# Strassen's block product for half of an output projection, with VectorE making the remainders of its weights

## The chip, the cores and the metric

The kernel runs on one core of a Trainium2 chip. The metric is the device time of one execution in microseconds (us), the median of several executions. All tensors are float32. "TensorE" does the matmuls (PE in the profile), "VectorE" is DVE, "ScalarE" is ACT, "GpSimd" is POOL, "SyncE" (SP) issues the loads and stores of this kernel.

## The reference

One layer of a hybrid mixer over 512 tokens of width 2048: a norm, one input projection of 2048 by 7168, two groups of heads (a gated recurrence and a convolution, each giving 1024 channels), one output projection of 2048 by 2048, a norm of its result and the residual. The change touches the last two lines only.

```python
h = rmsnorm(x, pre_norm_g[l])
proj = jnp.einsum('btd,dn->btn', h, w_in[l])
q, fz, iv, gate_a, u, ug, gate_b = jnp.split(proj, split_pts, axis=-1)
o_a = hgrn2_mixer(q, fz, iv, lower_bounds[l], hg_norm_g[l]) * jax.nn.silu(gate_a)
o_b = conformer_conv(u, ug, dw_kernel[l], dw_bias[l], conv_ln_g[l], conv_ln_b[l]) * jax.nn.silu(gate_b)
mixed = jnp.concatenate([o_a, o_b], axis=-1)          # (1, 512, 2048)
y = jnp.einsum('btm,md->btd', mixed, w_out[l])        # w_out: (2048, 2048)
x = x + rmsnorm(y, post_norm_g[l])
```

## The kernel before

Every engine has a program of its own, written out in order; the engines wait for each other on semaphores (`wait_ge(sem, n)`), and nothing is reordered.

**Products in three parts.** To keep float32 accuracy each operand of a projection is split in a rounded part (`hi`, type fp32r) and the remainder (`lo = value - hi`), and each product is made of three matmuls: hi by hi, hi by lo, lo by hi.

**Units of weights.** The weights of both projections come in units of 128 partitions by 1024 elements (512 KB). A unit n goes through a ring of four slots in three tensors: SyncE loads `w_raw`, ScalarE copies it into `w_hi` (`hi_unit`, L386, which waits for the load and for the unit n - 4 to be used up, `unit_done`), GpSimd makes `w_lo = w_raw - w_hi` (`lo_unit`, L333, `lo_done`), and TensorE uses both. SyncE's load of unit n waits for `lo_done` of unit n - 4.

**The output projection** goes over four chunks c of 512 columns of `w_out`, and in each over eight units s (`OUT_U`), each with 256 of the 2048 mixed channels (in the order of `PAIRS`, the channels that are ready first coming first). A unit is 24 matmuls of 128 rows, 128 channels and 512 columns (`out_products`): four tiles tt of 128 tokens, two channel blocks, three matmuls. Chunk c is summed in PSUM banks 4 * (c % 2) + tt. The last four units of the last chunk are gone through tile by tile, so that tile 0 is whole first.

**The left operand** is made during chunk 0: the mixed channels lie in `mix`, transposed (channels on the partitions, 512 tokens along), ScalarE rounds them block by block into `h_hi` (`mix_hi`, L625) and VectorE makes `h_lo` (`mix_lo`, L1022, `mlo_done`). Unit s of chunk 0 waits for `mlo_done` of 2s + 2 blocks. Between them VectorE still works on the last head and the last convolution tile: `late(H - 1, ...)` and `ln_tile`; the last block of `mix`, which is head 7, comes out of `late` at s == 7 (L990, L993), so the chain L990, L993, `mix_hi(15)`, `mix_lo(15)` ends just ahead of unit 7 of chunk 0.

**After a chunk** ScalarE squares and sums each bank (`take_sq`, L636, `y_sq`) and VectorE writes the bank times the norm's gain into `mix` (`take_y`, L1032). After the last chunk, for each tile in turn: ScalarE squares; VectorE adds the four sums (L1053) and does `take_y`; ScalarE makes the root (L672, L674); VectorE writes y * root + x over the tile (L1059, one instruction of 2048 columns, in the last tile four of 512); SyncE stores it (1 MB, the last tile in four parts).

Of the kernel before, what the change touches and what calls it, by code (L numbers as in the profile page):

```python
# [27 lines left out]
def build_layer(nc, x, pre_norm_g, post_norm_g, w_in, lb_logits, hg_norm_g, dw_kernel, dw_bias,  # L28
# [3 lines left out]
    ds = bass.ds  # L32
# [59 lines left out]
    with ctx:  # L92
# [16 lines left out]
        def part(n, k=1):  # L109
            return work[:, n * T:(n + k) * T]  # L110
# [49 lines left out]
        def h_pair(h, th, k):  # L160
# [74 lines left out]
        def _(sp):  # L235
            def load_unit(n, slot, src, width):
                sp.dma_start(w_raw[:, slot * UW:(slot + 1) * UW].rearrange("p (k c) -> p k c", c=width),
                             src.rearrange("(k p) c -> p k c", p=P)).then_inc(raw_in[slot], 16)
# [49 lines left out]
            with sp.Fori(0, H) as h:  # L288
                for u in range(HEAD_U):
# [4 lines left out]
                    in_unit(n, u % RING, u % 2, HEAD_COLS[u // 2] + h * P)  # L294
            with sp.Fori(0, CHUNKS) as c:
                for s in range(OUT_U):
                    n = N_OUT + OUT_U * c + s
                    cut_before = held(sp, n - RING + 1)
                    sp.wait_ge(raw_in[s % RING], 16)
                    sp.wait_ge(lo_done, cut_before)  # L300
                    load_unit(n, s % RING, w_out[0, 2 * P * PAIRS[s]:2 * P * (PAIRS[s] + 1), ds(c * 512, 512)], 512)
            parts = 0
# [9 lines left out]
        def _(pool):  # L312
# [55 lines left out]
            g.memset(probs, 0.0).then_inc(masks_ready, 1)  # L368
            with pool.Fori(PEEL, N_END // RING) as i:
                for s in range(RING):  # L370
                    lo_unit(RING * i + s, s)


        @block.scalar
        def _(act):
# [250 lines left out]

            def take_sq(c, tt):


                if c < CHUNKS - 1:  # L630
                    act.wait_ge(y_taken, TT * c + tt + 1)
                else:
                    act.wait_ge(y_mm, (TT - 1) * c + tt + 1)
                if c:
                    act.wait_ge(y_sq, TT * (c - 1) + tt + 1)
                A(part(tt), bank(4 * (c % 2) + tt), ACT.Square, accum_out=ssq[:, tt * CHUNKS + c:tt * CHUNKS + c + 1]).then_inc(y_sq, 1)  # L636

            def out_hi(c, s):
                n = N_OUT + OUT_U * c + s + AHEAD
                if n < N_END:  # L640
                    hi_unit(n, n % RING, n // RING)
# [16 lines left out]
            for c in range(1, CHUNKS):  # L658
                for s in range(OUT_U):
                    out_hi(c, s)  # L660
                    if c == 1 and s == 0:

                        act.wait_ge(mlo_done, KT)
                        for tt in range(TT):
                            act.dma_start(work[:, 4 * T + tt * D:4 * T + (tt + 1) * D], x[0, tt * P:(tt + 1) * P, :]).then_inc(res_in, 16)
                    if s in (1, 2):
                        take_sq(c - 1, 2 * s - 2)
                        take_sq(c - 1, 2 * s - 1)
# [9 lines left out]
        def _(dve):  # L678
# [344 lines left out]

            def take_y(c, tt):

                if c == CHUNKS - 1:
                    dve.wait_ge(y_sq, TT * c + tt + 1)
                elif tt < TT - 1:
                    dve.wait_ge(y_mm, (TT - 1) * c + tt + 1)
                else:  # L1030
                    dve.wait_ge(unit_done, N_OUT + OUT_U * (c + 1))
                V.tensor_tensor(mix[:, tt * D + c * 512:tt * D + (c + 1) * 512], bank(4 * (c % 2) + tt),  # L1032
                                gates[:, c * 512:(c + 1) * 512], ALU.mult).then_inc(y_taken, 1)

            for at in range(4):
                mix_lo(at)
            for s in range(OUT_U):
# [6 lines left out]
                for at in {2: (6, 7), 3: (8, 9), 4: (10, 11), 5: (12, 13), 6: (14,), 7: (15,)}.get(s, ()):  # L1044
                    mix_lo(at)
            dve.wait_ge(gain_in, 32)
            for c in range(CHUNKS - 1):
                for tt in range(TT):
                    take_y(c, tt)
            dve.wait_ge(res_in, 16 * TT)  # L1050
            for tt in range(TT):
                dve.wait_ge(y_sq, TT * (CHUNKS - 1) + tt + 1)
                V.tensor_reduce(rst[:, TT + tt:TT + tt + 1], ssq[:, tt * CHUNKS:(tt + 1) * CHUNKS], AX.X, ALU.add).then_inc(y_ssum, 1)  # L1053
                take_y(CHUNKS - 1, tt)
                dve.wait_ge(y_rs, 2 * (tt + 1))
                dve.wait_ge(y_taken, TT * (CHUNKS - 1) + tt + 1)
                for a, b in out_parts(tt):
                    y = mix[:, tt * D + a:tt * D + b]
                    V.scalar_tensor_tensor(y, y, rst[:, tt:tt + 1], work[:, 4 * T + tt * D + a:4 * T + tt * D + b],  # L1059
                                           ALU.mult, ALU.add).then_inc(y_out, 1)  # L1060


        @block.tensor
        def _(pe):
# [221 lines left out]

            def out_products(c, s, tt):
                for k in range(2):
                    a = slice((2 * s + k) * T + tt * P, (2 * s + k) * T + (tt + 1) * P)
                    w = slice((s % RING) * UW + k * 512, (s % RING) * UW + (k + 1) * 512)  # L1290
                    o = bank(4 * (c % 2) + tt)
                    mm(o, h_hi[:, a], w_hi[:, w], start=s == 0 and k == 0, stop=False)  # L1292
                    mm(o, h_hi[:, a], w_lo[:, w], start=False, stop=False)  # L1293
                    ins = mm(o, h_lo[:, a], w_hi[:, w], start=False, stop=s == OUT_U - 1 and k == 1)  # L1294
                return ins

            for c in range(CHUNKS):
                for s in range(OUT_U):
                    n = N_OUT + OUT_U * c + s
                    if N_END - n <= RING:  # L1300
                        break
                    if c == 0:
                        slot(H - 1, s, False, last=True)
                    if c == 0 and s == 0:
                        pe.wait_ge(gb_taken, H)
                    if s == 0 and c >= 2:
                        pe.wait_ge(y_sq, TT * (c - 1))
                    pe.wait_ge(lo_done, n + 1)
                    if c == 0:
                        pe.wait_ge(mlo_done, 2 * s + 2)  # L1310
                    for tt in range(TT):
                        if (c, s, tt) == (0, 0, 1):
                            pe.wait_ge(gate_taken, H)
                        ins = out_products(c, s, tt)
                        if s == OUT_U - 1 and tt < TT - 1:
                            ins.then_inc(y_mm, 1)
                    ins.then_inc(unit_done, 1)

            for tt in range(TT):
                for s in range(OUT_U - RING, OUT_U):  # L1320
                    pe.wait_ge(lo_done, N_END - OUT_U + s + 1)
                    ins = out_products(CHUNKS - 1, s, tt)
                ins.then_inc(y_mm, 1)
# [22 lines left out]
```

## Time and profile before

| | |
|---|---|
| three timed executions | 880.49, 880.89, 882.67 us; median 880.89 us |
| the profiled execution | 880.39 us, of which its span on the core is 878.4 us |
| TensorE busy | 867.4 us, 99% of the span |
| VectorE, ScalarE, GpSimd busy | 558.2 us, 389.5 us, 364.2 us |
| chain that ended last | TensorE 99% |

The span is the time between the first and the last recorded instruction or transfer; 2 us of the device's time lie outside it. A busy share is an average over stages: in the output projection VectorE is nearly unused between the chunks.

### The profile page before, as it was taken

The numbers are of one execution on the slowest core, as the hardware profiler recorded it, in microseconds if no ns is written. First come the engines' busy times: TensorE is split into PE (matmuls) and PEld (weight loads), VectorE is DVE, ScalarE is ACT, GpSimd is POOL, SyncE is SP. The second block draws the span as 40 slices with busy tenths as digits, with TensorE's granted clock in tenths as the row PEclk, the third lists the DMA queues.
The fourth block names the chain that finished last, engine by engine and source line by source line (L and its number), as shares of the span: only waits on it lengthen the run. The fifth ranks groups of instructions, "written<-read, shape, count | busy, mean of one in ns | idle before, by whom it ended". The sixth has DMA issues, their size and how long they took to land.

```text
span 878.4 us, 12378 instructions
## 1 busy us (share of the span) xinstructions
PE 867.4 (99%) x4258; PEld 727.5 (83%) x4258; DVE 558.2 (64%) x929; ACT 389.5 (44%) x617; POOL 364.2 (41%) x165
## 2 busy tenths in 40 slices
PE   8999999999999999999999999999999999999996
PEld 7988888888888888888888888888888888888885
DVE  4697788788678993957758395775939882010105
ACT  7522213323323466646646564664656653222221
POOL 4284444444444444342524434253443443444440
PEclk9999999999999999999999999999999999999998
DMA  9253333333333323141331324133131336433304
GB/s 311 80 145 98 97 99 101 97 101 100 97 98 98 95 64 97 58 121 49 96 96 51 105 59 119 48 96 96 48 105 62 110 131 234 143 99 99 96 1 191
DMA packets 115899, 89.76 MB, mean 102 GB/s; under 512 B 2672, under 2 KB 101273, under 8 KB 114585
## 3 DMA queue, kind: packets, MB, share of 16 engines
q1 hardware_dynamic: 115113, 84.04, 31.5%
q10 hardware_dynamic: 752, 5.25, 1.6%
q8 instruction: 23, 0.38, 0.2%
q14 instruction: 11, 0.09, 0.0%
HBM read 85.09 MB, written 4.19 MB: 102 GB/s over the span
## 4 chain that ended last, share of the span: by engine, by line
PE 99%; DVE 0%; ACT 0%; POOL 0%; issue 0%; DVEq 0%; ACTq 0%; POOLq 0%
PE banks L1155 19%; PE banks L1157 19%; PE banks L1156 19%; PE banks L1292 7%; PE banks L1293 7%; PE banks L1294 7%; PE banks L1170 3%; PE banks L1171 3%; PE banks L1172 3%; PE banks L1101 3%; PE banks L1213 1%; PE banks L1203 1%; PE banks L1219 1%; PE banks L1072 1%; PE banks L1247 1%; PE banks L1222 1%
## 5 line engine op out<-in xcount | busy, mean ns | idle before, releaser
L333 POOL TENSOR_TENSOR w_lo<-w_raw,w_hi 128x1024 fp32r<-128x1024 f32 x144 | 358.1, 2490 | 487.3 <-ACT w_hi L386 486.9
L1155 PE MATMUL banks<-h_hi,w_hi 128*128 128x512 f32 x736 | 291.1, 396 | 0.0
L1157 PE MATMUL banks<-h_hi,w_lo 128*128 128x512 f32 x736 | 286.7, 390 | 0.0
L1156 PE MATMUL banks<-h_lo,w_hi 128*128 128x512 f32 x736 | 286.5, 389 | 0.0
L386 ACT ACTIVATE w_hi<-w_raw 128x1024 fp32r<-128x1024 f32 x144 | 151.9, 1055 | 263.5 <-PE banks L1294 100.1
L745 DVE SCALAR_TENSOR_TENSOR banks<-work,tap,banks 128x512 f32<-128x512 f32 x232 | 175.3, 756 | 8.0
L1157 PEld LDWEIGHTS banks<-h_hi,w_lo 128*128 128x128 f32 x736 | 138.1, 188 | 29.3
L1156 PEld LDWEIGHTS banks<-h_lo,w_hi 128*128 128x128 f32 x736 | 138.3, 188 | 28.1 <-issue 0.5
L1155 PEld LDWEIGHTS banks<-h_hi,w_hi 128*128 128x128 f32 x736 | 138.2, 188 | 28.0 <-issue 0.5
L1292 PE MATMUL banks<-w_hi,h_hi 128*128 128x512 f32 x256 | 100.6, 393 | 0.0
L1294 PE MATMUL banks<-w_hi,h_lo 128*128 128x512 f32 x256 | 99.7, 389 | 0.0
L1293 PE MATMUL banks<-w_lo,h_hi 128*128 128x512 f32 x256 | 99.6, 389 | 0.0
L1032 DVE TENSOR_TENSOR mix<-banks,gates 128x512 f32<-128x512 f32 x16 | 11.0, 689 | 85.6 <-PE banks L1294 85.6
L1294 PEld LDWEIGHTS banks<-w_hi,h_lo 128*128 128x128 f32 x256 | 48.0, 188 | 10.1
L1292 PEld LDWEIGHTS banks<-w_hi,h_hi 128*128 128x128 f32 x256 | 48.1, 188 | 10.1 <-issue 0.2
L1293 PEld LDWEIGHTS banks<-w_lo,h_hi 128*128 128x128 f32 x256 | 48.1, 188 | 10.0 <-issue 0.2
L1170 PE MATMUL banks<-w_hi,h_hi 128*128 128x512 f32 x128 | 49.8, 389 | 0.0
L1171 PE MATMUL banks<-w_lo,h_hi 128*128 128x512 f32 x128 | 49.8, 389 | 0.0
L1172 PE MATMUL banks<-w_hi,h_lo 128*128 128x512 f32 x128 | 49.8, 389 | 0.0
L946 DVE COPY_PREDICATED work<-mask,banks 128x192 f32<-128x192 int8 (+2 forms) x48 | 14.6, 303 | 27.5 <-PE banks L1213 20.2
L1172 PEld LDWEIGHTS banks<-w_hi,h_lo 128*128 128x128 f32 x128 | 24.0, 188 | 5.0
L1170 PEld LDWEIGHTS banks<-w_hi,h_hi 128*128 128x128 f32 x128 | 24.0, 188 | 5.0
(180 smaller groups left out, 906.2 us busy)
## 6 DMA issues: line engine op xcount, KB each, us to landing
w_raw<-in_w_in SPq DMA_DIRECT2D x112, 512.0 KB, 3.7
w_raw<-in_w_out SPq DMA_DIRECT2D x32, 512.0 KB, 3.7
work<-in_x ACTq DMA_DIRECT2D x4, 1024.0 KB, 10.0
out_y<-mix SPq DMA_DIRECT2D x3, 1024.0 KB, 3.9
mix<-in_x SPq DMA_DIRECT2D x4, 512.0 KB, 5.3
mix<-in_x SPq DMA_DIRECT2D x2, 1024.0 KB, 9.7
gates<-in_post_norm_g ACTq DMA_DIRECT2D x1, 1024.0 KB, 5.7
out_y<-mix SPq DMA_DIRECT2D x4, 256.0 KB, 2.7
```

Of the source, the lines that this page charges most:

```text
L333: g.tensor_tensor(w_lo[:, a], w_raw[:, a], w_hi[:, a].bitcast(fp32), ALU.subtract).then_inc(lo_done, 1)
L386: A(w_hi[:, a], w_raw[:, a], ACT.Copy).then_inc(hi_done, 1)
L745: V.scalar_tensor_tensor(dst, src, tp[:, w:w + 1], acc, ALU.mult, ALU.add).then_inc(tap_done, 1)
L1155: mm(bank(b), wh, hh, start=kt == 0, stop=False)
L1156: mm(bank(b), wh, hl, start=False, stop=False)
L1157: ins = mm(bank(b), wl, hh, start=False, stop=kt == KT - 1)
L1170: mm(o, h_hi[:, a], w_hi[:, w], start=vu == 0 and k == 0, stop=False)
L1171: mm(o, h_hi[:, a], w_lo[:, w], start=False, stop=False)
L1172: ins = mm(o, h_lo[:, a], w_hi[:, w], start=False, stop=vu == 2 * VH - 1 and k == VK - 1)
L1292: mm(o, h_hi[:, a], w_hi[:, w], start=s == 0 and k == 0, stop=False)
L1293: mm(o, h_hi[:, a], w_lo[:, w], start=False, stop=False)
L1294: ins = mm(o, h_lo[:, a], w_hi[:, w], start=False, stop=s == OUT_U - 1 and k == 1)
```

## The change

Columns 0 to 511 (chunk 0) are done as before, with GpSimd's remainders. Columns 512 to 1023 are ordinary too (units `C0` to `C7`). For columns 1024 to 2047 the product of `mixed` (512 tokens by 2048 channels) and `w_out` (2048 by 1024) is cut in two by two blocks and done with seven block products instead of eight (`P1` to `P7`, in Winograd's form with sums that are reused): each has 256 tokens, 1024 channels and 512 columns, and four steps u of 12 matmuls. `STEPS` sets the order: P1 (4 steps), C0, P2 (4), P5 (4), then for P6, P7, P3, P4 in turn two steps, one C, two steps, and last C5, C6, C7, again tile by tile. P products are summed in banks 4 and 5 or 6 and 7, C in banks 0 to 3.

New work around it: `sum_sides` (VectorE, in place on `mix`, 12 instructions, 9 of them inside chunk 0) makes the sums of the left operand; `side_rounded` (ScalarE) and `side_rest` (VectorE) split them; `sum_weights` (VectorE, 16) makes the sums of weights in four buffers `bsum` or in `w_raw`; `fast_rest` (VectorE) makes `w_lo` for all steps but the first two, in GpSimd's place; `keep` (ScalarE) and `join`, L1308 (VectorE) add up the block products; `gain` multiplies. Four more loads of 512 KB bring the first weights for `bsum` during chunk 0. The residual x is loaded later, at P4, over `mix`. The final write of a tile is four instructions of 512 columns for all tiles.

The core of the diff:

```diff
+    STEPS = [("P1", u) for u in range(HU)] + [("C", 0)] + [("P2", u) for u in range(HU)] + [("P5", u) for u in range(HU)]
+    for at, kind in enumerate(("P6", "P7", "P3", "P4")):
+        STEPS += [(kind, 0), (kind, 1), ("C", at + 1), (kind, 2), (kind, 3)]
+    LAST_C = [("C", s) for s in range(5, OUT_U)]
+    STEPS += LAST_C
+    SUM_PARTS = ((0, 4), (4, 2), (6, 2))
...
+            act.wait_ge(joined, JOINED["c21"])
+            for tt in (0, 1):
+                square(2, 2 + tt, pair_c21[:, tt * 512:(tt + 1) * 512])
             for tt in range(TT):
-                take_sq(CHUNKS - 1, tt)
+                act.wait_ge(y_mm, TT - 1 + tt + 1)
+                square(1, tt, bank(tt))
+            for tt in range(TT):
                 act.wait_ge(y_ssum, tt + 1)
                 A(rst[:, tt:tt + 1], rst[:, TT + tt:TT + tt + 1], ACT.Ln, scale=1.0 / D, bias=EPSB).then_inc(y_rs, 1)
...
+            def sum_sides(n, at):
+                i, k = SUM_PARTS[at]
+                if n == 0:
+                    out, a, b, op = low(i, k, EARLY), low(i, k, EARLY), low(i, k, LATE), ALU.subtract
...
+                dve.wait_ge(mlo_done, i + k + (KT // 2 if n else 0))
+                if n:
+                    dve.wait_ge(m_summed, M_SUM[n - 1, at])
+                V.tensor_tensor(out, a, b, op).then_inc(m_summed, 1)
...
+            def fast_rest(m):
+                kind, u = STEPS[m]
+                src = bsum[u] if kind in ("P5", "P6", "P4") else raw_of((kind, u))
+                a = slice(m % RING * UW, (m % RING + 1) * UW)
+                dve.wait_ge(hi_done, N_FAST + m + 1)
+                V.tensor_tensor(w_lo[:, a], src, w_hi[:, a].bitcast(fp32), ALU.subtract).then_inc(fast_lo, 1)
...
                 for at in {2: (6, 7), 3: (8, 9), 4: (10, 11), 5: (12, 13), 6: (14,), 7: (15,)}.get(s, ()):
                     mix_lo(at)
+                if s == 4:
+                    for at in range(3):
+                        sum_sides(0, at)
+                    for n in (1, 2, 3):
+                        sum_sides(n, 0)
+                if s == 6:
+                    for n in (1, 2, 3):
+                        sum_sides(n, 1)
+            for m, (kind, u) in enumerate(STEPS):
+                if m + 1 < len(STEPS) and STEPS[m + 1][0] in AHEAD_SUM:
+                    sum_weights(*STEPS[m + 1])
+                if (kind, u) in SIDE:
+                    side_rest(kind, u)
+                if m >= 2:
+                    fast_rest(m)
...
             for tt in range(TT):
                 dve.wait_ge(y_sq, TT * (CHUNKS - 1) + tt + 1)
                 V.tensor_reduce(rst[:, TT + tt:TT + tt + 1], ssq[:, tt * CHUNKS:(tt + 1) * CHUNKS], AX.X, ALU.add).then_inc(y_ssum, 1)
-                take_y(CHUNKS - 1, tt)
+                take_y(1, tt, y1[:, tt * 512:(tt + 1) * 512], bank(tt))
                 dve.wait_ge(y_rs, 2 * (tt + 1))
...
-                for a, b in out_parts(tt):
+                for c, y in enumerate(y_parts(tt)):
+                    out_c = mix[:, tt * D + c * 512:tt * D + (c + 1) * 512]
+                    ins = V.scalar_tensor_tensor(out_c, y, rst[:, tt:tt + 1], out_c, ALU.mult, ALU.add)
...
+            for m, (kind, u) in enumerate(STEPS[:-len(LAST_C)]):
+                pe.wait_ge(lo_done, N_FAST + m + 1) if m < 2 else pe.wait_ge(fast_lo, m - 1)
```

VectorE's program in chunk 0, before. The first row is the end of the last convolution tile; L1022 are `mix_lo` of blocks 10 to 14 and, in the row behind L993, 15; L990 and L993 end head 7; L1032 takes chunk 0 out of PSUM.

```order
L825 TENSOR_TENSOR mix<-work 128x512 [waits ln_v,ln_sig]
L1022 TENSOR_TENSOR h_lo<-mix,h_hi 128x512 [waits mhi_done] x5
L990 TENSOR_TENSOR work<-banks,work 128x512 [waits rs_s]
L993 SCALAR_TENSOR_TENSOR mix<-work,par 128x512 [waits gate_ready,on_done]
L1022 TENSOR_TENSOR h_lo<-mix,h_hi 128x512 [waits mhi_done]
L1032 TENSOR_TENSOR mix<-banks,gates 128x512 [waits y_mm,gain_in]
L1032 TENSOR_TENSOR mix<-banks,gates 128x512 [waits y_mm] x2
L1032 TENSOR_TENSOR mix<-banks,gates 128x512 [waits unit_done]
```

The same place now. L980 is the old L825, L1177 the old L1022, L1145 and L1148 the old L990 and L993; L1200 is `sum_sides`, L1215 `sum_weights` for P1, L1241 `fast_rest`.

```order
L980 TENSOR_TENSOR mix<-work 128x512 [waits ln_v,ln_sig]
L1177 TENSOR_TENSOR h_lo<-mix,h_hi 128x512 [waits mhi_done] x2
L1200 TENSOR_TENSOR mix<-mix 128x4x256 [waits mlo_done]
L1200 TENSOR_TENSOR mix<-mix 128x2x256 [waits mlo_done] x2
L1200 TENSOR_TENSOR mix<-mix 128x4x256 [waits m_summed,mlo_done] x3
L1177 TENSOR_TENSOR h_lo<-mix,h_hi 128x512 [waits mhi_done] x3
L1200 TENSOR_TENSOR mix<-mix 128x2x256 [waits m_summed,mlo_done] x3
L1145 TENSOR_TENSOR work<-banks,work 128x512 [waits rs_s]
L1148 SCALAR_TENSOR_TENSOR mix<-work,par 128x512 [waits gate_ready,on_done]
L1177 TENSOR_TENSOR h_lo<-mix,h_hi 128x512 [waits mhi_done]
L1215 TENSOR_TENSOR work<-work,w_raw 128x1024 [waits raw_in0,first_in0,lo_done]
```

Six sums now stand ahead of `mix_lo` of blocks 12 to 14, and three more ahead of the end of head 7.

ScalarE's program at its end, before (two of the four tiles; L636 squares, L672 and L674 make the root):

```order
L636 ACTIVATE work,ssq<-banks 128x512 [waits y_sq,y_mm]
L672 ACTIVATE rst<-rst,epsb 128x1 [waits y_ssum]
L674 ACTIVATE rst<-rst 128x1 [waits y_rs]
L636 ACTIVATE work,ssq<-banks 128x512 [waits y_sq,y_mm]
L672 ACTIVATE rst<-rst,epsb 128x1 [waits y_ssum]
```

The same place now (L733 squares, L827 and L829 make the root):

```order
L733 ACTIVATE near,ssq<-work 128x512 [waits y_sq,joined]
L733 ACTIVATE near,ssq<-work 128x512 [waits y_sq]
L733 ACTIVATE near,ssq<-banks 128x512 [waits y_sq,y_mm] x4
L827 ACTIVATE rst<-rst,epsb 128x1 [waits y_ssum]
L829 ACTIVATE rst<-rst 128x1 [waits y_rs]
L827 ACTIVATE rst<-rst,epsb 128x1 [waits y_ssum]
```

The squares of all four tiles now stand ahead of the first tile's root.

## Rows read from the trace of the kernel before

**Rows 1.** The page: the chain that ended last, by engine.

```profile
PE 99%; DVE 0%; ACT 0%; POOL 0%; issue 0%; DVEq 0%; ACTq 0%; POOLq 0%
```

**Rows 2.** Timeline of ScalarE: start us, us, instruction [idle before <-releaser].

```profile
728.56 1.06 ACT L386 ACTIVATE w_hi<-w_raw 128x1024 fp32r<-128x1024 f32 x1 [4.95 <-PE banks L1294]
...
732.76 0.63 ACT L625 ACTIVATE h_hi<-mix 128x512 fp32r<-128x512 f32 x1 [1.90 <-DVE mix L993]
...
762.11 1.06 ACT L386 ACTIVATE w_hi<-w_raw 128x1024 fp32r<-128x1024 f32 x1 [4.38 <-PE banks L1294]
767.55 1.06 ACT L386 ACTIVATE w_hi<-w_raw 128x1024 fp32r<-128x1024 f32 x1 [4.38 <-PE banks L1294]
```

**Rows 3.** Timeline of TensorE: units 6 and 7 of chunk 0, and the end.

```profile
729.40 0.40 PE L1293 MATMUL banks<-w_lo,h_hi 128*128 128x512 f32 x1
...
734.65 0.39 PE L1292 MATMUL banks<-w_hi,h_hi 128*128 128x512 f32 x1
...
740.09 0.39 PE L1292 MATMUL banks<-w_hi,h_hi 128*128 128x512 f32 x1
...
870.42 0.39 PE L1294 MATMUL banks<-w_hi,h_lo 128*128 128x512 f32 x1
```

**Rows 4.** Timeline of VectorE in chunk 0.

```profile
697.82 2.88 DVE L962 TENSOR_TENSOR work<-work 128x512 f32<-128x512 f32 x1
...
716.75 5.30 DVE L1022 TENSOR_TENSOR h_lo<-mix,h_hi 128x512 fp32r<-128x512 f32 x5
730.89 0.69 DVE L990 TENSOR_TENSOR work<-banks,work 128x512 f32<-128x512 f32 x1 [8.84 <-ACT work L587]
731.62 1.04 DVE L993 SCALAR_TENSOR_TENSOR mix<-work,par 128x512 f32<-128x512 f32 x1
733.42 0.69 DVE L1022 TENSOR_TENSOR h_lo<-mix,h_hi 128x512 fp32r<-128x512 f32 x1 [0.76 <-ACT h_hi L625]
```

**Rows 5.** Timeline of GpSimd in chunk 0.

```profile
697.30 2.84 POOL L333 TENSOR_TENSOR w_lo<-w_raw,w_hi 128x1024 fp32r<-128x1024 f32 x1
...
717.21 2.49 POOL L333 TENSOR_TENSOR w_lo<-w_raw,w_hi 128x1024 fp32r<-128x1024 f32 x1 [2.90 <-ACT w_hi L386]
722.64 2.40 POOL L333 TENSOR_TENSOR w_lo<-w_raw,w_hi 128x1024 fp32r<-128x1024 f32 x1 [2.94 <-ACT w_hi L386]
729.70 2.42 POOL L333 TENSOR_TENSOR w_lo<-w_raw,w_hi 128x1024 fp32r<-128x1024 f32 x1 [4.65 <-ACT w_hi L386]
```

**Rows 6.** Groups by line and shape from 700 us on: busy us, mean ns.

```profile
L1059 DVE SCALAR_TENSOR_TENSOR mix<-mix,rst,work 128x2048 f32<-128x2048 f32 x3 | 7.1, 2351 | 0.3
...
L1059 DVE SCALAR_TENSOR_TENSOR mix<-mix,rst,work 128x512 f32<-128x512 f32 x4 | 2.7, 747 | 0.1
```

**Rows 7.** Timeline of ScalarE at the end, last tile.

```profile
870.85 0.60 ACT L636 ACTIVATE work<-banks 128x512 f32<-128x512 f32 x1 [4.00 <-PE banks L1294]
...
871.76 0.29 ACT L672 ACTIVATE rst<-rst,epsb 128x1 f32<-128x1 f32 x1 [0.23 <-DVE rst L1053]
```

**Rows 8.** Timeline of VectorE at the end, last two tiles.

```profile
866.98 2.35 DVE L1059 SCALAR_TENSOR_TENSOR mix<-mix,rst,work 128x2048 f32<-128x2048 f32 x1
871.57 0.16 DVE L1053 TENSOR_REDUCE rst<-ssq 128x1 f32<-128x4 f32 x1 [2.23 <-ACT work L636]
...
872.43 2.74 DVE L1059 SCALAR_TENSOR_TENSOR mix<-mix,rst,work 128x512 f32<-128x512 f32 x4
```

**Rows 9.** Landings of the residual's four loads (L665), then of weights (L237), 720 to 760 us.

```profile
DMA to landing us min/median/max: 5.0/10.0/14.0
...
DMA to landing us min/median/max: 3.6/3.8/10.5
```

**Rows 10.** Stretches: length, busy us of PE (matmuls), PEld, DVE, ACT, POOL, granted clock, DMA.

```profile
2.00:4.00 2.00, 2.00 (x11) 2.00 (x10) 0.14 (x1) 0.10 (x1) 0.06 (x1) 1.00 0.84 242
...
6.00:7.00 1.00, 1.00 (x12) 1.00 (x11) 0.00 (x0) 0.90 (x2) 0.00 (x0) 1.00 0.94 344
...
872.50:873.00 0.50, 0.00 (x0) 0.00 (x0) 0.50 (x1) 0.00 (x0) 0.00 (x0) 0.81 0.14 49
```

More of the change, by code:

```diff
@@ L125, in build_layer @@
         glu = kdec
+        pair_c11, pair_c22 = part(0, 2), part(2, 2)
+        bsum = [part(4 + 2 * u, 2) for u in range(HU)]
+        pair_c21 = part(16, 2)
+        sides = sb("sides", [P, 2 * SIDES * T], fp32r)
+        side_hi = [sides[:, 2 * r * T:(2 * r + 1) * T] for r in range(SIDES)]
+        side_lo = [sides[:, (2 * r + 1) * T:(2 * r + 2) * T] for r in range(SIDES)]
+        y1 = part(12, TT)
+        pair_c12 = part(18, 2)
+        y0 = gates[:, D:2 * D]
         grow = work[0:KT, 0:P]
@@ L638, in out_hi, with square @@
[L638 to L641, printed above, removed]
+            squares = [0]
+            def square(c, tt, y):
+                if squares[0]:
+                    act.wait_ge(y_sq, squares[0])
+                squares[0] += 1
+                A(near[:, 0:512], y, ACT.Square, accum_out=ssq[:, tt * CHUNKS + c:tt * CHUNKS + c + 1]).then_inc(y_sq, 1)
+            def out_hi(s):
+                n = N_OUT + s + AHEAD
+                if n < N_FAST:
+                    hi_unit(n, n % RING, n // RING)
+                else:
+                    fast_hi(n - N_FAST)
@@ new lines, in side_rounded, with keep @@
+            def side_rounded(kind, u):
+                i = SIDE[kind, u]
+                act.wait_ge(m_summed, M_SUM[SUM_OF[kind], max(0, u - 1)])
+                if i >= SIDES:
+                    prev = [step for step in SIDE if SIDE[step] == i - SIDES][0]
+                    act.wait_ge(unit_done, N_FAST + AT[prev] + 1)
+                A(side_hi[i % SIDES].rearrange("p (k t) -> p k t", k=2), side(kind, u), ACT.Copy).then_inc(side_his, 1)
+            def keep(step, pair, b):
+                act.wait_ge(unit_done, N_FAST + AT[step] + 1)
+                A(pair, bank(b, 2), ACT.Copy).then_inc(kept, 1)
@@ new lines, in join, with gain @@
+            def join(step, out, b, pair, joins=0):
+                dve.wait_ge(unit_done, N_FAST + AT[step] + 1)
+                if joins:
+                    dve.wait_ge(joined, joins)
+                for n in range(2):
+                    a = slice(n * 512, (n + 1) * 512)
+                    V.tensor_tensor(out[:, a], bank(b + n), pair[:, a], ALU.add).then_inc(joined, 1)
+            def gain(c, pair, sq):
+                dve.wait_ge(y_sq, sq)
+                dve.wait_ge(gain_in, 32)
+                for n in range(2):
+                    a = slice(n * 512, (n + 1) * 512)
+                    take_y(c, n, pair[:, a], pair[:, a])
@@ L1293, in out_products @@
                     mm(o, h_hi[:, a], w_lo[:, w], start=False, stop=False)
-                    ins = mm(o, h_lo[:, a], w_hi[:, w], start=False, stop=s == OUT_U - 1 and k == 1)
+                    ins = mm(o, h_lo[:, a], w_hi[:, w], start=False, stop=last and k == 1)
                 return ins
[L1297 to L1310, printed above, removed]
-                    for tt in range(TT):
[L1312 to L1316, printed above, removed]
-                    ins.then_inc(unit_done, 1)
@@ new lines, in _ @@
+            for s in range(OUT_U):
+                n = N_OUT + s
+                slot(H - 1, s, False, last=True)
+                if s == 0:
+                    pe.wait_ge(gb_taken, H)
+                pe.wait_ge(lo_done, n + 1)
+                pe.wait_ge(mlo_done, 2 * s + 2)
+                for tt in range(TT):
+                    if (s, tt) == (0, 1):
+                        pe.wait_ge(gate_taken, H)
+                    ins = out_products(s % RING, s, tt, s == 0, s == OUT_U - 1)
+                    if s == OUT_U - 1 and tt < TT - 1:
+                        ins.then_inc(y_mm, 1)
+                ins.then_inc(unit_done, 1)
@@ new lines, in fast_products @@
+            def fast_products(kind, u, m):
+                b = 4 if kind in ("P1", "P5", "P7", "P4") else 6
+                for n in range(2):
+                    for k in range(2):
+                        if kind in ("P1", "P2", "P4"):
+                            at, tt = 2 * u + k + (0 if kind == "P1" else KT // 2), n + (2 if kind == "P4" else 0)
+                            a = slice(at * T + tt * P, at * T + (tt + 1) * P)
+                            ah, al = h_hi[:, a], h_lo[:, a]
+                        else:
+                            r = SIDE[kind, u] % SIDES
+                            a = slice(k * 2 * P + n * P, k * 2 * P + (n + 1) * P)
+                            ah, al = side_hi[r][:, a], side_lo[r][:, a]
+                        w = slice(m % RING * UW + k * 512, m % RING * UW + (k + 1) * 512)
+                        first, last = u == 0 and k == 0, u == HU - 1 and k == 1
+                        mm(bank(b + n), ah, w_hi[:, w], start=first, stop=False)
+                        mm(bank(b + n), ah, w_lo[:, w], start=False, stop=False)
+                        ins = mm(bank(b + n), al, w_hi[:, w], start=False, stop=last)
+                ins.then_inc(unit_done, 1)
```

260 lines of the change are left out of this document (209 added, 51 removed).

## The prediction

> **What bounds the kernel now.** First the chain that ended last: 99% of it is TensorE [rows 1], so what TensorE no longer has to do comes off the span, if nothing new makes it wait. Then the end of that chain: the last matmul starts at 870.42 us and takes 0.39, so it ends at 870.81, and the span of 878.4 has 7.6 us behind it, which are ScalarE, VectorE and a store [rows 3, 7, 8]. Last the timelines of chunk 0, the place where the other engines are fullest: they show how close VectorE's work is to TensorE's need. `mix_lo(15)` ends at 733.42 + 0.69 = 734.11 and unit 7 of chunk 0, which waits for it, starts at 734.65 [rows 3, 4]. That is 0.54 us of slack. Three places decide: the matmuls saved, chunk 0, and the tail.
>
> **The matmuls.** One unit of 24 matmuls takes 767.55 - 762.11 = 5.44 us by ScalarE's copies, each of which TensorE releases [rows 2]; from the first matmul behind unit 7 (740.09 us less the one started 734.65 gives 5.44 again) to the last of all there are 24 units, 130.56 us. A pace of 5.44 / 24 = 0.227 us each. Now there are 8 ordinary units and 28 steps of half a unit: 8 x 5.44 + 28 x 2.72 = 119.68 us. **Saved: 48 matmuls, 10.9 us.** The left operands now partly come from another tensor, with the same shape and form, so I keep the pace.
>
> **Do the steps starve?** VectorE now makes the remainders. Its two-input instruction takes 0.69 us for 512 elements [rows 4]; from 512 to 2048 elements the final write goes from 0.747 to 2.351 us, 1.044 ns for an element [rows 6], so 1024 elements take 0.69 + 0.53 = 1.22 us. The fullest stretch is P6 and P7 with their two C units: 10 remainders, 8 sums of weights and the sum at L1308 at 1.22 each (23.2), 8 side remainders, two joins and two gains at 0.69 (8.3): 31.5 us against 2 x (4 x 2.72 + 5.44) = 32.6 us of TensorE. Full, but it fits, and the ring lets VectorE run up to three steps ahead. I followed the four queues step by step with these durations and 1.06 us for ScalarE's copy [rows 2]: no step waits, the thinnest spots are C2 (weights ready about 0.5 us early) and C0 (over 1 us: the third remainder comes at the end of chunk 0, then one sum, four takes of 0.69, the last square, copy and remainder, 9 us in all, against 10.9 us of P1). Loads: each raw slot has over 3 us beyond the 3.8 us of a landing. The residual's 4 MB took 14.0 us until the last had landed and pushed a weight load to 10.5 us [rows 9]; at P4 they are issued over 20 us ahead of the tail, and the last weights have a few us to spare. So I cost the loads and the steps at nothing; if that cover is gone it costs what the last rival says.
>
> **Chunk 0.** VectorE gets nine sums in front of `mix_lo(12)` to (14) and of L990. Four have 1024 elements and five 512: 4 x 1.22 + 5 x 0.69 = 8.3 us. VectorE was idle for 8.84 us ahead of L990 [rows 4], so by busy time they would just fit. But GpSimd's remainders run in the same stretch, and a two-input VectorE instruction doesn't run beside them: L962 began at 697.82 and took 2.88 us instead of 0.69, until 0.56 us after GpSimd's instruction of 697.30 ended at 700.14; and the five L1022 from 716.75 took 5.30 us, five times 0.6 and the 2.3 that GpSimd's of 717.21 was still running [rows 4, 5]. They take turns. So laid down one by one: block 11 ends at 720.3; three sums to 722.6; a fourth to 723.75, where GpSimd's next (asked for at 722.64) gets its turn, 2.4 us; two more sums to 728.6; blocks 12 and 13 to 729.75. Unit 6, which needs block 13, began its products at 729.4 - 0.23 = 729.2 [rows 3]: 0.6 us late. Then block 14, GpSimd's instruction of 729.70 until 732.65 (ScalarE's copy at 728.56 releases it [rows 2]), three dependent sums to 734.7, L990 and L993 (1.04) to 736.4, and from L993's end to block 15's it was 734.11 - 732.66 = 1.45 us with ScalarE's copy in between [rows 2, 4]: 737.9. Unit 7 needs that at 735.2 and started at 734.65 before. **Lost: 3.3 us.** Behind L990 nothing but this chain waits. Bounds: nothing, if the two do not exclude each other for these; 4.0 us, if block 13 too falls behind GpSimd's turn.
>
> **The tail.** Before, a tile's square, root and final write lie under the next tile's matmuls; only the last tile's are bare. From the end of the last matmul (870.81) to the last tile's writes is 872.43 - 870.81 = 1.62 us, the four writes take 2.74, and from their end at 875.17 to the span's end it is 3.2 us [rows 7, 8]. Now ScalarE has all four squares ahead of the first root, and the fourth waits for the last matmul. So no root, and no final write, comes before the last matmul has ended. Tile 0's writes start a bit sooner after it (its reduction is done, 0.2 us less: 1.4), then 2.74. For each of the other three, VectorE's reduction, ScalarE's root and the start of the writes take 872.43 - 871.57 = 0.86 us [rows 7, 8], since they stand behind the writes of the tile before, and then 2.74, less 0.1 where they overlap: 3.5. In all 1.4 + 2.74 + 3 x 3.5 = 14.7 us against 4.36. **Lost: 10.3 us.** The stores of tiles 0 to 2 lie under the next tile's writes; the end stays at 3.2 us. Bounds: with writes of 0.61 us each, the pace of L1022, it is 1.2 us less; with a store held up behind the one before, perhaps 1 us more.
>
> **Sum.** -10.9 + 3.3 + 10.3 = +2.7 us, and 0.1 for small waits: the span goes from 878.4 to 881.2, the profiled execution from 880.39 to 883.2. The median of the three timed runs lies 0.5 us above that execution, so I give 883.7 for a median, 0.32% slower. A measurement of this kernel tells about 0.3% from no change, 2.6 us; the forecast lies at that edge, on the slow side of it, with 1 us of its own to either side (882.7 to 884.7).
>
> **Rivals.**
> - *Chunk 0 hides the sums.* For it: 8.84 us of idle time against 8.3 us of work. Against it: both L962 and the five L1022. The place is the stretch from 716.75 to 734.65; it decides whether GpSimd's two instructions (4.8 us) block VectorE. If neither does, the loss falls to 0, and the sum is -0.6: 880.3, no change. With one of them it is about 1.7 - 0.5 = 1.2 us, 881.6. Chance 0.18.
> - *The clock falls.* TensorE now stands still for 2.5 us ahead of unit 7. At the end of the run the granted clock fell within 872.50 to 873.00 (mean 0.81 of it), 2.0 us after the last matmul had ended [rows 10]. So it may fall to the lower level, 1.2 GHz, in chunk 0. At the start TensorE did 11 matmuls of the warm-up in 2 us and later 12 in 1 us [rows 10]; the change came some 4 us after it began. Four us at half speed cost 2 us more: 885.5 (1 to 2 us more by where it falls). Against it: the pause is only 0.5 us longer than the time after which the clock fell there. Chance 0.15. [...]
> - *VectorE or the loads starve the steps.* Margins of 0.5 us at C2 and 1.1 us in P6 and P7 are thin. A 1024-element instruction of 1.35 us instead of 1.22 costs 19 x 0.13 = 2.5 us there, less the 1.1: 1.4 us; a residual that took 25 us in place of its 14.0 [rows 9] would make C6 and C7 wait for some 4 us. For it: a stretch that is 97% full. Together +1 to +4: 886. Chance 0.15.
> - *The tail is not bare, or cheaper.* Some of the tail's 10.3 us is not lost, and the kernel comes out under 878.2. It needs 5 us less than summed, against an order of instructions that is plain. Chance 0.05.
>
> **How the numbers follow.** My forecast 0.47, of which a little over half lies above +0.3% (883.5) and the rest below: 0.27 and 0.20. Slower: 0.27 + 0.15 + 0.15 = 0.57. Same: 0.20 + 0.18 = 0.38. Faster: 0.05. The range for 8 in 10 goes from 880.2 (the first rival) to 886.8 (the second whole, the third in part).
>
> **What the profile after would show.** Right: gaps of TensorE ahead of units 6 and 7 of chunk 0, some 0.6 and 2.6 us, released by VectorE's L1177; sums (L1200) of about 1.2 us, and one or two of over 3 us beside GpSimd; hardly a gap from P1 to the last C; the last matmul near 863; then four groups of four writes, 3.5 us apart, and ScalarE's roots all behind the last square. The granted clock stays at 1.00 until then. Wrong: a TensorE without gaps in chunk 0 (first rival), a clock of 0.5 behind the gap (second), TensorE's gaps released by `w_lo` (third), a final write ahead of the last matmul's end (fourth).

## The result, and the profile after

The changed kernel takes 890.22 us (median of 4 runs, 889.95 to 891.47) against 880.74 us: a ratio of 1.0106, 95% interval 1.0088 to 1.0123. It is 9.5 us slower. The forecast was slower too, but 2.8 us, with 883.7 us and a range up to 886.8: the direction was right, the size was not, and the range missed it. The profiled execution has a span of 888.2 us, 9.8 more than before.

The page first: busy time by engine, and the chain that ended last, which answers to [rows 1].

```profile
PE 858.7 (97%) x4210; PEld 720.1 (81%) x4210; DVE 648.5 (73%) x1029; ACT 413.8 (47%) x648; POOL 311.9 (35%) x143
...
PE 94%; DVE 3%; issue 1%; DMA 1%; ACT 0%; DVEq 0%; POOL 0%; SPq 0%; ACTq 0%; POOLq 0%
```

TensorE has 48 matmuls fewer, but is no longer 99% of the chain. The timeline of TensorE shows where it stood (start, duration, instruction, in brackets the idle time before it); it answers to [rows 3]:

```profile
728.64 1.02 PE L1524 MATMUL banks<-work,ones 128*128 128x512 f32 x2
737.07 0.77 PE L1562 MATMUL banks<-w_hi,h_hi 128*128 128x512 f32 x1 [7.41 <-DVE h_lo L1177]
737.63 0.63 PE L1563 MATMUL banks<-w_lo,h_hi 128*128 128x512 f32 x1
738.06 0.63 PE L1564 MATMUL banks<-w_hi,h_lo 128*128 128x512 f32 x1
738.48 0.63 PE L1562 MATMUL banks<-w_hi,h_hi 128*128 128x512 f32 x1
...
740.52 0.39 PE L1564 MATMUL banks<-w_hi,h_lo 128*128 128x512 f32 x1
...
749.61 0.39 PE L1597 MATMUL banks<-w_hi,h_hi 128*128 128x512 f32 x1
...
869.11 0.39 PE L1564 MATMUL banks<-w_hi,h_lo 128*128 128x512 f32 x1
```

One gap of 7.41 us ahead of unit 6, released by `mix_lo` (L1177), where 0.6 and 2.6 us at two places had been laid down. Behind it matmuls start 0.43 us apart for some 3 us, nearly twice the 0.227 of the full pace. The granted clock of these stretches (the third column from the end: 0.86, 0.50, 0.96; 1.00 is 2.4 GHz, 0.50 the lower level, 1.2 GHz) says why:

```profile
730.00:735.00 5.00, 0.00 (x0) 0.00 (x0) 4.79 (x3) 1.16 (x2) 3.30 (x2) 0.86 0.22 86
735.00:740.00 5.00, 2.93 (x7) 2.38 (x8) 4.79 (x8) 0.00 (x0) 0.00 (x0) 0.50 0.00 0
740.00:745.00 5.00, 5.00 (x22) 4.10 (x22) 4.04 (x5) 1.20 (x2) 0.00 (x0) 0.96 0.02 6
```

P1's first matmul starts at 749.61; the matmul behind chunk 0 started at 740.09 before [rows 3], so chunk 0 lost 9.5 us (0.3 of it had been there already at L1524: 728.64 against 728.30 for the same matmuls before). From there to the start of a matmul behind the last, 869.11 + 0.23, it is 119.7 us: to the tenth what 28 steps and 8 units were to take, without a gap. The timelines of VectorE and GpSimd in chunk 0, which answer to [rows 4, 5]:

```profile
717.37 2.48 DVE L980 TENSOR_TENSOR mix<-work 128x512 f32<-128x512 f32 x1 [5.19 <-ACT work L602]
719.77 1.28 DVE L1177 TENSOR_TENSOR h_lo<-mix,h_hi 128x512 fp32r<-128x512 f32 x2
720.97 14.74 DVE L1200 TENSOR_TENSOR mix<-mix 128x1024 f32<-128x1024 f32 x6
735.63 1.89 DVE L1177 TENSOR_TENSOR h_lo<-mix,h_hi 128x512 fp32r<-128x512 f32 x3
737.44 2.28 DVE L1200 TENSOR_TENSOR mix<-mix 128x512 f32<-128x512 f32 x3
```

```profile
716.90 2.40 POOL L430 TENSOR_TENSOR w_lo<-w_raw,w_hi 128x1024 fp32r<-128x1024 f32 x1 [16.41 <-ACT w_hi L485]
721.97 2.46 POOL L430 TENSOR_TENSOR w_lo<-w_raw,w_hi 128x1024 fp32r<-128x1024 f32 x1 [2.67 <-ACT w_hi L485]
724.70 8.61 POOL L430 TENSOR_TENSOR w_lo<-w_raw,w_hi 128x1024 fp32r<-128x1024 f32 x3 [0.27 <-ACT w_hi L485]
```

Six sums took 14.74 us, for 6.2 us of own work, because GpSimd made four remainders in this stretch, three of them in a row, where one was forecast. Taken singly, a sum that meets one of them is recorded at about 3 us and ends 0.55 us behind it (1.09 us if it has 1024 elements), about the sum's own work. The second sum, whose 2.87 us end at 724.98 while GpSimd's remainder of 721.97 ends at 724.43:

```profile
722.11 2.87 DVE L1200 TENSOR_TENSOR mix<-mix 128x512 f32<-128x512 f32 x1
```

GpSimd had been idle for 16.41 us before: its work had been late. ScalarE's copy that released it had waited for a load, and the loads' queue shows who held them. ScalarE's row first, then SyncE's timeline, then its line in the list of waits (line waited for, us, times, longest):

```profile
715.76 1.06 ACT L485 ACTIVATE w_hi<-w_raw 128x1024 fp32r<-128x1024 f32 x1 [7.79 <-DMA w_raw<-in_w_out]
```

```profile
681.07 0.37 SPq L312 DMA_DIRECT2D w_raw<-in_w_out  x1
710.12 0.37 SPq L384 DMA_DIRECT2D work<-in_w_out  x1
710.59 0.42 SPq L312 DMA_DIRECT2D w_raw<-in_w_out  x1
```

```profile
SPq L384 <- PE banks L1492: 22.0, 1, 22.0
```

SyncE stood for 22 us at `sp.wait_ge(lev_done, 4 * H)` ahead of the first load into `bsum` (and for 6.6 us before that at `qdec_ready`). L1492 is the last head's own matmul in unit 3 of chunk 0. The loads of units 5 to 7 and of P1 were queued behind that wait: unit 5's was issued at 710.59, and at 686.90 in the kernel before. It is the wait and not the bytes that held them: from 682 to 709 us the DMA engines were 7% busy, against 31% before. (Let go all at once, the weights then landed 8.1 us behind their issue in the median, against 3.7 before.)

The tail, VectorE and ScalarE, answers to [rows 7, 8]; the last matmul ends at 869.11 + 0.39 = 869.50:

```profile
858.16 0.68 DVE L1181 TENSOR_TENSOR work<-banks,gates 128x512 f32<-128x512 f32 x1
870.68 0.75 DVE L1328 SCALAR_TENSOR_TENSOR mix<-gates,rst,mix 128x512 f32<-128x512 f32 x1 [11.83 <-ACT rst L829]
871.35 2.07 DVE L1328 SCALAR_TENSOR_TENSOR mix<-work,rst,mix 128x512 f32<-128x512 f32 x3
873.33 0.15 DVE L1322 TENSOR_REDUCE rst<-ssq 128x1 f32<-128x4 f32 x1
...
881.87 2.07 DVE L1328 SCALAR_TENSOR_TENSOR mix<-work,rst,mix 128x512 f32<-128x512 f32 x3
```

```profile
869.54 0.60 ACT L733 ACTIVATE near<-banks 128x512 f32<-128x512 f32 x1 [3.39 <-PE banks L1564]
...
870.13 0.28 ACT L827 ACTIVATE rst<-rst,epsb 128x1 f32<-128x1 f32 x1
```

VectorE waited 11.83 us for tile 0's root, which ScalarE made only behind the square of tile 3. Writes end at 883.94, 14.4 us behind the last matmul (14.7 were forecast), and the span ends 4.3 us later, against 3.2 before. In all 18.7 us against 7.6: 11.1 lost. The sum of the span: -10.8 + 9.5 + 11.1 = +9.8 us.

### The profile page after: what moved, and what is told of

Same layout as the page of the kernel before. It is cut to its first block, busy times and chain, and to the rows that moved or that the text cites. A ratio compares the mean times of both kernels' runs of the same rounds, so it can differ in the third digit from the quotient of the medians.

```text
span 888.2 us, 12341 instructions
## 1 busy us (share of the span) xinstructions
PE 858.7 (97%) x4210; PEld 720.1 (81%) x4210; DVE 648.5 (73%) x1029; ACT 413.8 (47%) x648; POOL 311.9 (35%) x143
## 4 chain that ended last, share of the span: by engine, by line
PE 94%; DVE 3%; issue 1%; DMA 1%; ACT 0%; DVEq 0%; POOL 0%; SPq 0%; ACTq 0%; POOLq 0%
PE banks L1425 19%; PE banks L1427 19%; PE banks L1426 19%; PE banks L1440 3%; PE banks L1442 3%; PE banks L1441 3%; PE banks L1598 3%; PE banks L1599 3%; PE banks L1597 3%; PE banks L1562 3%; PE banks L1371 3%; PE banks L1563 3%; PE banks L1564 3%; DVE mix L1200 1%; PE banks L1473 1%; PE banks L1483 1%
## 5 line engine op out<-in xcount | busy, mean ns | idle before, releaser
L430 POOL TENSOR_TENSOR w_lo<-w_raw,w_hi 128x1024 fp32r<-128x1024 f32 x122 | 305.8, 2510 | 420.3 <-ACT w_hi L485 419.8
L1562 PE MATMUL banks<-w_hi,h_hi 128*128 128x512 f32 x128 | 51.3, 400 | 7.4 <-DVE h_lo L1177 7.4
L1563 PE MATMUL banks<-w_lo,h_hi 128*128 128x512 f32 x128 | 50.4, 394 | 0.0
L1564 PE MATMUL banks<-w_hi,h_lo 128*128 128x512 f32 x128 | 50.3, 393 | 0.0
L1440 PE MATMUL banks<-w_hi,h_hi 128*128 128x512 f32 x128 | 49.8, 389 | 0.0
L1441 PE MATMUL banks<-w_lo,h_hi 128*128 128x512 f32 x128 | 49.8, 389 | 0.0
L1442 PE MATMUL banks<-w_hi,h_lo 128*128 128x512 f32 x128 | 49.8, 389 | 0.0
L1241 DVE TENSOR_TENSOR w_lo<-w_raw,w_hi 128x1024 fp32r<-128x1024 f32 x22 | 26.7, 1222 | 13.1 <-ACT w_hi L757 13.1
L1562 PEld LDWEIGHTS banks<-w_hi,h_hi 128*128 128x128 f32 x128 | 24.4, 191 | 13.2 <-issue 8.2
L757 ACT ACTIVATE w_hi<-w_raw 128x1024 fp32r<-128x1024 f32 x24 | 24.9, 1054 | 21.4 <-PE banks L1564 10.7
L922 DVE SCALAR_TENSOR_TENSOR work<-banks,work 128x512 f32<-128x512 f32 x8 | 5.5, 692 | 32.1 <-ACT work L493 32.1
L1086 DVE COPY_PREDICATED work<-mask,banks 128x256 f32<-128x256 int8 x16 | 11.9, 743 | 23.3 <-PE banks L1473 22.5
L1564 PEld LDWEIGHTS banks<-w_hi,h_lo 128*128 128x128 f32 x128 | 24.4, 191 | 5.3
```

Source lines behind the costliest of these rows:

```text
L430: g.tensor_tensor(w_lo[:, a], w_raw[:, a], w_hi[:, a].bitcast(fp32), ALU.subtract).then_inc(lo_done, 1)
L1440: mm(o, h_hi[:, a], w_hi[:, w], start=vu == 0 and k == 0, stop=False)
L1442: ins = mm(o, h_lo[:, a], w_hi[:, w], start=False, stop=vu == 2 * VH - 1 and k == VK - 1)
L1562: mm(o, h_hi[:, a], w_hi[:, w], start=first and k == 0, stop=False)
L1564: ins = mm(o, h_lo[:, a], w_hi[:, w], start=False, stop=last and k == 1)
```

## The experiments

The theory after the result: three things add up, each with its own place: (1) SyncE's queue, held by the wait for `bsum`, delays the weights so that GpSimd's remainders fall on VectorE's sums; (2) the gap lets the clock fall; (3) ScalarE's order bares the tail. All kernels start from the changed one; the edits are shown cut to their core. The ratios are to the kernel before, measured beside them on the same chip (880.75 us for e_load, e_sums, e_tail and e_all, 880.61 us for the other three).

**e_load: the loads into `bsum`, and the wait, behind those of chunk 0.**

```diff
                 load_unit(n, s % RING, w_out[0, out_rows(s), 0:512], 512)
-                if s >= HU:
-                    u = s - HU
+            for u in range(HU):
                     if u == 0:
                         sp.wait_ge(lev_done, 4 * H)
```

> Changed kernel with the four loads into bsum, and SyncE's wait for lev_done and qdec_ready ahead of them, moved behind the load of unit 7 of chunk 0. Theory (SyncE stood 22 us at that wait, units 5 to 7 and the first two of P1 came late, and GpSimd's remainders fell together with VectorE's sums): the gap ahead of unit 6 shrinks from 7.4 us to under 1 us and one of about 2.6 us opens ahead of unit 7, as the prediction laid down; 884 us, or 885.5 if the clock falls all the same. Rival (the nine sums alone make the gap, whenever the weights come): it stays at 6 us or more, 889 to 890 us.

Measured: 884.99 us (883.88 to 885.34), ratio 1.0044 (1.0030 to 1.0059), 5.2 us below the changed kernel. TensorE's gaps in chunk 0:

```profile
730.32 0.47 PE L1561 MATMUL banks<-w_hi,h_hi 128*128 128x512 f32 x1 [0.43 <-DVE h_lo L1176]
...
738.17 0.47 PE L1561 MATMUL banks<-w_hi,h_hi 128*128 128x512 f32 x1 [2.12 <-DVE h_lo L1176]
```

That is the picture of the prediction (0.6 and 2.6 us), and in this execution (884.12 us) the granted clock stays at 1.00 there:

```profile
735.00:740.00 5.00, 2.88 (x13) 2.12 (x12) 4.21 (x6) 1.58 (x2) 0.00 (x0) 1.00 0.00 0
```

Three of the five executions took 885.0 to 885.3 us at a mean granted clock of 0.990, two 883.9 and 884.1 us at 0.991, so the clock may have fallen for a while in the three; no trace shows them. The whole difference between forecast and result in chunk 0 hung on SyncE's wait. The gaps that are left are the sums' and GpSimd's.

**e_sums: the wait stays, the nine sums go behind chunk 0** (six behind `mix_lo(15)`, three to P2).

```diff
-                if s == 4:
-                    for at in range(3):
-                        sum_sides(0, at)
-                    for n in (1, 2, 3):
-                        sum_sides(n, 0)
-                if s == 6:
-                    for n in (1, 2, 3):
-                        sum_sides(n, 1)
+            for at in range(3):
+                sum_sides(0, at)
+            for n in (1, 2, 3):
+                sum_sides(n, 0)
...
                 if (kind, u) == ("P2", 0):
+                    for n in (1, 2, 3):
+                        sum_sides(n, 1)
```

> Changed kernel with the nine sums of the left operand that stood inside chunk 0 moved behind mix_lo(15): six there, three to P2. SyncE's wait stays. Theory (the sums stand ahead of mix_lo(13), and without them nobody waits): no gap over 1 us in chunk 0 and a clock of 1.00; about 881 us. Rival (late weights starve TensorE in chunk 0 by themselves): the time stays near 889 us, with gaps released by w_lo.

Measured: 884.59 us (884.36 to 885.41), ratio 1.0040 (1.0025 to 1.0054). Chunk 0 has no gap: late weights alone starve nobody. The result was 3.6 us above what I expected. Six sums now push VectorE's four takes of chunk 0 and with them ScalarE's squares (e_best tests this), and a new gap opens at C0, a spot whose margin the prediction had called thin:

```profile
755.73 0.50 PE L1560 MATMUL banks<-w_hi,h_hi 128*128 128x512 f32 x1 [1.85 <-DVE w_lo L1241]
```

That explains 1.9 us of the 3.6, and 1 us is the longer end behind the writes, which the expectation had left out. That leaves 0.7 us in the median and 1.5 in the traced execution (885.41 us). The latter ran at the lower clock for over 3 us near its start, long before the change; at half the pace that costs about half the time:

```profile
18.00:21.00 3.00, 3.00 (x15) 3.00 (x15) 2.22 (x6) 2.27 (x6) 1.52 (x2) 0.50 1.02 371
```

The other four executions have the same mean granted clock, 0.989, but no trace shows where theirs fell. Behind the gap of 1.85 us at C0 it stayed at 1.00 here.

**e_load_nopool: as e_load, and GpSimd's last two remainders made by VectorE behind chunk 0.**

```diff
-            for n in (N_FAST, N_FAST + 1):
-                lo_unit(n, n % RING)
...
-                if m >= 2:
-                    fast_rest(m)
+                fast_rest(m)
```

> The kernel with the loads moved (e_load) and, besides, GpSimd's last two remainders (units P1,0 and P1,1, its instructions of 723 and 730 us) made by VectorE behind chunk 0. The sums stay where they are. Theory (VectorE's two-input instructions and GpSimd's exclude each other, and these two block the sums): the gaps of 0.4 and 2.1 us go, VectorE has 8.3 us of sums in 8.8 us of idle time; 885.0 less 2.5: 882.5 us. Rival (the sums' own length and place make the gaps): they stay, 885 us or more, since VectorE has two remainders more.

Measured: 880.97 us (880.52 to 881.23), ratio 0.9997 (0.9988 to 1.0006): 4.0 us below e_load, where 2.5 were expected. Between the two traced executions (884.12 and 881.14 us) it is 3.0; the last us lies between e_load's traced execution and its median. No gap of TensorE is left in chunk 0, with the sums where the change had put them; VectorE's rows there:

```profile
720.67 6.21 DVE L1197 TENSOR_TENSOR mix<-mix 128x1024 f32<-128x1024 f32 x6
726.80 1.89 DVE L1174 TENSOR_TENSOR h_lo<-mix,h_hi 128x512 fp32r<-128x512 f32 x3
728.60 2.27 DVE L1197 TENSOR_TENSOR mix<-mix 128x512 f32<-128x512 f32 x3
731.40 0.69 DVE L1142 TENSOR_TENSOR work<-banks,work 128x512 f32<-128x512 f32 x1 [0.52 <-ACT work L683]
```

The six sums take 6.21 us here, 8.23 in e_load and 14.74 in the changed kernel, the same instructions each time. They fit in the idle time with 0.5 us over. So the first rival, that chunk 0 hides the sums, is exactly what happens once GpSimd is out of the way of the sums. The Trainium skill, SBUF — State Buffer, section "SBUF: two separate sides", states it as a lock: of a VectorE instruction with two inputs in SBUF and a GpSimd instruction that reads SBUF, the one that starts first holds the shared ports for the whole instruction and the other is blocked. The rows of the changed kernel agree in that every sum that met a GpSimd instruction ended its own 0.55 or 1.09 us behind that instruction; the record of the sum counts the wait in, so the two overlap in the timeline.

**e_warm: idle matmuls in the gap.** 30 matmuls of 512 columns into a free bank ahead of the wait of unit 6.

```diff
+                if s == 6:
+                    for i in range(30):
+                        mm(LV0, h_hi[:, 0:P], w_hi[:, 0:512], start=True, stop=True)
                 pe.wait_ge(lo_done, n + 1)
```

> Changed kernel with 30 idle matmuls of 512 columns into a free bank ahead of the wait of unit 6 in chunk 0 (some 6.8 us at the full pace, inside the gap of 7.4 us); nothing of the result changes. Theory (the clock fell to the lower level in the gap, and the first matmuls behind it ran at 0.43 us each): the granted clock stays at 1.00, unit 6 runs at 0.227 us a matmul, and 1.5 us come back: 888.7 us. Rival (the slow matmuls come from something else than the gap): no change, 890.2 us.

Measured: 888.65 us (888.31 to 889.10), ratio 1.0087 (1.0069 to 1.0105), 1.6 us below the changed kernel, as expected. The gap is filled, the next matmuls run at 0.227 us:

```profile
729.10 7.41 PE L1574 MATMUL banks<-w_hi,h_hi 128*128 128x512 f32 x30
736.86 0.47 PE L1562 MATMUL banks<-w_hi,h_hi 128*128 128x512 f32 x1 [0.34 <-DVE h_lo L1177]
737.17 0.39 PE L1563 MATMUL banks<-w_lo,h_hi 128*128 128x512 f32 x1
```

and the granted clock is 1.00 up to the last matmul. VectorE still releases unit 6 at the same place (L1177), 0.2 us sooner than in the changed kernel, so this is the price of the clock by itself.

**e_tail: each root behind its own square.**

```diff
                 square(1, tt, bank(tt))
-            for tt in range(TT):
                 act.wait_ge(y_ssum, tt + 1)
```

> Changed kernel with one edit at its end: ScalarE makes each tile's root right behind its square again, instead of all four squares first. Theory (the squares ahead of the roots push all final writes behind the last matmul): the end from the last matmul to the span's end falls from 18.7 us to about 7.6 us, the time from 890.2 to about 879.1 us. Rival (VectorE's own work for a tile, 3.5 us against 4.08 us of matmuls, can't keep up even so): 2 to 4 us of it stay, 881 to 883 us.

Measured: 879.52 us (878.77 to 882.62), ratio 0.9985 (0.9971 to 0.9999): 10.7 us below the changed kernel by one line. Seven of the ten executions took 878.8 to 879.7 us and three 882.5 to 882.6; the traced one is of the three (882.59 us). It ran at the lower clock near its start, like e_sums's, and around the gap of chunk 0 for some 10 us, against 6.8 in the changed kernel (both by the granted clocks of the stretches):

```profile
18.00:21.00 3.00, 3.00 (x15) 3.00 (x15) 2.26 (x6) 2.31 (x6) 1.51 (x2) 0.50 1.00 376
734.00:746.00 12.00, 6.90 (x18) 5.50 (x19) 10.89 (x13) 0.63 (x1) 1.34 (x1) 0.57 0.00 0
```

That is most of the 3.2 us by which its last matmul comes later than the changed kernel's. Tiles 0 and 3:

```profile
862.17 0.75 DVE L1327 SCALAR_TENSOR_TENSOR mix<-gates,rst,mix 128x512 f32<-128x512 f32 x1
...
874.34 0.75 DVE L1327 SCALAR_TENSOR_TENSOR mix<-gates,rst,mix 128x512 f32<-128x512 f32 x1
875.01 2.07 DVE L1327 SCALAR_TENSOR_TENSOR mix<-work,rst,mix 128x512 f32<-128x512 f32 x3
```

Its last matmul ends at 872.72, so tile 0's writes begin 10.5 us ahead of it, and the span (880.7 us) ends 8.0 us behind it, where 7.6 were expected. VectorE keeps up with the tiles (3.5 us of work in 4.08), so the rival fell.

**e_all and e_best: all of it together.** e_all has the edits of e_tail, e_load and e_sums. e_best has those of e_tail and e_load; of its twelve sums of the left operand five stand in VectorE's idle time ahead of the end of head 7, one behind `mix_lo(15)` and six at P2 (three of these were there already).

```diff
-                if s == 4:
+                if s == 6:
                     for at in range(3):
                         sum_sides(0, at)
-                    for n in (1, 2, 3):
+                    for n in (1, 2):
                         sum_sides(n, 0)
-                if s == 6:
-                    for n in (1, 2, 3):
-                        sum_sides(n, 1)
+            sum_sides(3, 0)
...
                 if (kind, u) == ("P2", 0):
+                    for n in (1, 2, 3):
+                        sum_sides(n, 1)
```

> All three edits together. If matmuls saved, chunk 0 and tail add up: 880.7 before less 10.9, plus at most 1 us for small waits: 870 to 871 us. Rival (the block product costs more elsewhere, once those two are gone; VectorE is 97 per cent full in P6 and P7): over 873 us.

> Tail and loads as in e_all; of the sums, five stand ahead of the end of head 7, where VectorE was idle, one behind mix_lo(15), the other six at P2. Theory (e_all's 1.9 us gap at C0 was caused by six sums pushing VectorE's takes of chunk 0, and part of its runs lost 2 us more to the clock): no gap, all runs alike at 870 to 871 us, 10 us below before. Rival (the gap at C0 comes from ScalarE's chain of squares and copies, whatever VectorE does): a gap of about 1 us or more stays, 872 us.

Measured: e_all 873.98 us (871.86 to 874.14), ratio 0.9912 (0.9892 to 0.9931), above its expectation and past the rival's 873, though the steps starve nowhere but at C0. Its trace has the gap there again, 1.86 us up to 753.47, and this time the clock fell, some 0.9 us after the matmuls had resumed. Two stretches, with the granted clock in the column of 0.59 and 0.56:

```profile
754.00:756.00 2.00, 2.00 (x7) 1.52 (x6) 1.84 (x3) 2.00 (x4) 0.00 (x0) 0.59 0.61 164
756.00:758.00 2.00, 2.00 (x7) 1.57 (x6) 1.84 (x3) 0.82 (x1) 0.00 (x0) 0.56 0.85 277
```

e_best: 870.34 us (869.75 to 872.24), ratio 0.9880 (0.9863 to 0.9898). TensorE has no gap in it from chunk 0 to its last matmul, so the sums' place made the gap at C0, and that rival fell. It is 10.3 us faster than the kernel before: the 10.9 us of the matmuls, nearly whole. That all runs would be alike did not come true: one of the five took 872.24 us, at a mean granted clock of 0.995 against 0.997 and 0.998.

## Why the prediction was wrong, step by step

- **The matmuls, -10.9 us: right.** 119.7 us measured for the steps and units, 119.68 forecast; e_best shows the gain whole.
- **The steps do not starve: right.** No gap from P1 to the end in the changed kernel. The 1024-element instruction takes 1.22 us (mean of L1241's 22), as worked out. The thin spot at C0 was real, and "over 1 us" the right size: from e_best to e_all the first take of chunk 0 moves by 3.1 us (744.36 to 747.47) and 1.9 of them become a gap, so some 1.2 us were to spare.
- **Chunk 0, "Lost: 3.3 us": the step that failed.** 9.5 us were lost. The prediction's list of the work beside the sums took GpSimd's instructions to stand where they stood before (one in the sums' way, at 722.64, and one at 729.70), and its step on loads ("I cost the loads and the steps at nothing") looked at landings and slots from P1 on. The four loads into `bsum` have no term in it, neither for their bytes nor for the wait in front of them. The runs showed that wait in its place: SyncE stood 22 us for `lev_done` with the weights of units 5 to 7 behind it, four of GpSimd's remainders fell on the six sums instead of one, and the sums took 14.74 us. With the wait moved (e_load) chunk 0 loses 3.0 us (P1 starts at 743.70, 3.6 us later than before, of which 0.6 us are there ahead of the gaps), against 9.2 in the changed kernel counted the same way, so the laid down sequence was right for the queue that it assumed.
- **"The clock falls", a rival at 0.15 with about 2 us: it came about**, in the longer gap, and cost 1.6 us (e_warm). In e_load's traced execution, with gaps of 0.4 and 2.1 us, it did not. (Its 885.5 adds 1.8 us to 883.7 where its text says 2.) The argument against this rival compared the pause with the 2.0 us of a single fall, the one at the end of the kernel before. The other traces give no such fixed time: in the changed kernel the engine had stood still for 3.9 us (729.66 to about 733.6, by the 0.86 above) before the clock fell, and in e_all it was at work again.
- **The tail, "Lost: 10.3 us": right in mechanism**, 11.1 us measured: 14.4 us to the last write's end, and some 1 us more than before from there to the span's end, which stood in the text as a bound ("a store held up behind the one before, perhaps 1 us more"). e_tail shows the cause; what holds the last store is not shown.
- **Sum.** Forecast +2.8 us of span, measured +9.8. Of the 7.0 us between them 6.2 lie in chunk 0 (9.5 against 3.3: 1.6 the clock's, 0.3 there before the gap, 4.3 more of waiting) and 0.8 in the tail. e_load, at 885.0 us, is about what the forecast of 883.7 describes, with the tail's last us added. That "slower" came true is no luck: it rested on the tail, and without the tail's loss the changed kernel is level with the one before (e_tail, 0.9985).

## What to carry to other kernels

A load that is added to a queue brings its wait with it: ask what that semaphore waits for and what stands behind it in the queue, before its bytes. Work that fits into an engine's idle time by its sum may still not fit, if another engine shares its way to SBUF: count that engine's instructions in the stretch as well, and ask whether the change moves them there. When a loop over tiles at the end of a kernel is split in two, everything of the second loop is bare behind the last matmul; a saving of 48 matmuls was worth as much as one line of order.

## What the runs showed of the hardware

- Delayed work on one engine came back as contention on another: a pause of 16.41 us of GpSimd, harmless by itself (e_sums has it too and no gap in chunk 0), made six VectorE instructions take 14.74 us instead of 6.21.
- A gap of TensorE of 1.86 us (e_all) was followed by the lower clock, and gaps of 1.85 us (e_sums) and 2.12 us (e_load) were not, each in the traced execution. Of the four runs of e_all one took 871.9 us at a mean granted clock of 0.997 and three 873.9 to 874.1 us at 0.995, so the price of such a gap seems to differ from run to run by about 2 us.
- In the traced executions of e_sums and e_tail the granted clock is 0.50 from 18 to 21 us, hundreds of us ahead of anything that the edits touch; e_tail's took 3 us more than seven of its fellows. The kernel before has executions of this kind too (four of 15 on either chip, 882.6 to 883.0 us, at a mean clock of 0.996 to 0.997 against 0.997 to 0.999). That they have the same cause isn't shown, as none of them was traced.
